# Value projections with the activations stationary, in a two-block transformer kernel

## The reference

```python
qkv = jnp.einsum('bsd,de->bse', x, w_qkv).reshape(b, s, 3, h, dh)
...
p = jax.nn.softmax(...)
return (... + jnp.einsum('bhqk,bhkd->bhqd', p_own, v_own))
```

## Time and profile before

| | |
|---|---|
| median of 3 runs | 819.25 us (818.97 to 820.73) |
| span of the profiled execution, first to last instruction | 817.3 us |
| median above the span | 1.95 us |
| TensorE busy (matmuls) | 802.3 us, 98% |
| VectorE busy | 644.4 us, 79% |
| ScalarE busy | 487.0 us, 60% |

### The profile page before, as it was taken

One profiled execution on the slowest core, in us unless ns is written; L12 is line 12 of the kernel. 1 busy time (PEld: TensorE's weight loads), 2 busy tenths in 40 slices (PEclk: granted clock), 3 DMA queues, 4 the chain that ended last, 5 costly groups with the idle time before them and its releaser, 6 DMA issues.

```text
span 817.3 us, 16917 instructions
## 1 busy us (share of the span) xinstructions
PE 802.3 (98%) x6862; PEld 780.7 (96%) x6862; DVE 644.4 (79%) x1333; ACT 487.0 (60%) x1015; POOL 21.2 (3%) x53
## 2 busy tenths in 40 slices
PE   7999999999999999999999999899999999999998
PEld 7999998999999999999999999889889999999998
DVE  5788887888899887999988786977667896775551
ACT  6754566767767565756554556665655775555440
POOL 1000000000000000000000000700000000000000
PEclk9999999999999999999999999999999999999999
DMA  8777673765565998489998887545334578665540
GB/s 290 260 234 226 200 267 128 235 199 188 189 225 166 324 308 286 144 295 336 361 333 292 288 263 222 167 134 175 120 118 156 156 249 274 207 199 194 194 155 27
DMA packets 150013, 179.44 MB, mean 220 GB/s; under 512 B 5680, under 2 KB 139568, under 8 KB 149936
## 3 DMA queue, kind: packets, MB, share of 16 engines
q1 hardware_dynamic: 147680, 177.22, 65.8%
q10 hardware_dynamic: 1232, 1.11, 0.4%
q0 software_dynamic: 1024, 0.03, 0.1%
HBM read 177.27 MB, written 1.05 MB: 218 GB/s over the span
## 4 chain that ended last, share of the span: by engine, by line
PE 77%; DVE 4%; ACT 2%; issue 1%; DVEq 0%; ACTq 0%
PE bank L1349 24%; PE bank L1352 24%; PE bank L1353 24%; DVE wlo L970 1%; PE bank L1451 1%; PE bank L1439 1%; PE bank L1468 0%; PE bank L1370 0%; PE bank L1402 0%; DVE yb L1010 0%; PE bank L1418 0%; DVE A L1021 0%; ACT B L748 0%; PE bank L1395 0%; ACT sq L768 0%
## 5 line engine op out<-in xcount | busy, mean ns | idle before, releaser
L970 DVE TENSOR_TENSOR wlo<-raw,whi 128x512 fp32r<-128x512 f32 x528 | 342.7, 683 | 69.4 <-ACT whi L727 68.7
L727 ACT ACTIVATE whi<-raw 128x512 fp32r<-128x512 f32 x528 | 307.3, 622 | 97.1 <-PE bank L1353 85.2
L1349 PE MATMUL bank<-A,whi 128*128 128x256 f32 x1264 | 357.3, 283 | 3.4 <-DVE wlo L970 2.6
L1352 PE MATMUL bank<-A,whi 128*128 128x256 f32 x1264 | 350.6, 277 | 0.1
L1353 PE MATMUL bank<-A,wlo 128*128 128x256 f32 x1264 | 350.2, 277 | 0.0
L1349 PEld LDWEIGHTS bank<-A,whi 128*128 128x128 f32 x1264 | 237.7, 188 | 6.5 <-DVE wlo L970 3.5
L1352 PEld LDWEIGHTS bank<-A,whi 128*128 128x128 f32 x1264 | 237.7, 188 | 1.2 <-issue 1.0
L1353 PEld LDWEIGHTS bank<-A,wlo 128*128 128x128 f32 x1264 | 237.8, 188 | 0.0
L1349 PE MATMUL bank<-Hhi,whi 128*128 128x256 f32 x528 | 146.2, 277 | 0.0
L1353 PE MATMUL bank<-Hhi,wlo 128*128 128x256 f32 x528 | 145.9, 276 | 0.0
L1352 PE MATMUL bank<-Hlo,whi 128*128 128x256 f32 x528 | 145.9, 276 | 0.0
(11 more groups left out here) (150 smaller groups left out, 811.0 us busy)
## 6 DMA issues: line engine op xcount, KB each, us to landing
mring<-in_w_mod SPq DMA_DIRECT2D x72, 512.0 KB, 6.4
raw<-in_ffn_w_up SPq DMA_DIRECT2D x22, 1024.0 KB, 5.1
raw<-in_w_gate SPq DMA_DIRECT2D x22, 1024.0 KB, 5.7
raw<-in_w_up SPq DMA_DIRECT2D x22, 1024.0 KB, 6.0
raw<-in_w_down SPq DMA_DIRECT2D x16, 1024.0 KB, 5.4
raw<-in_w_in SPq DMA_DIRECT2D x12, 1024.0 KB, 5.4
raw<-in_moba_w_qkv SPq DMA_DIRECT2D x11, 1024.0 KB, 5.5
raw<-in_ffn_w_down SPq DMA_DIRECT2D x8, 1024.0 KB, 6.2
```

The lines of the kernel that those rows point to most:

```text
L727: act.activation(whi[:, i % SPL, k0:k1, 0:width], raw[:, i % RAW, k0:k1, 0:width], ACT.Copy).then_inc(s_whi, 1)
L970: dve.tensor_tensor(lo, raw[:, i % RAW, k0:k1, 0:width], hi.bitcast(F32), ALU.subtract).then_inc(s_wlo, 1)
L1349: pe.matmul(o, hi, xh, start=kg == 0 and not (j and halved(g)), stop=False)
L1352: pe.matmul(o, hi, xl, start=False, stop=False)
```

## The change

The value groups are computed with the operands exchanged: the activations of 128 tokens are stationary and 256 columns of weights move, so that the result is token-major and VectorE evicts it straight into Vn. The step vturn is gone on both engines. In qkv1 the root of the norm is now needed as one number for each partition; root_columns gets it, once, as the diagonal of the broadcast root. In qkv3 the slabs at 1024 (sb values) and 1536 (first fox queries) change places, so that no value group is unnormed. The query group in fourth place is now the unnormed one.

```diff
-PAD_H = 168 - PAD_C
+PAD_H = 166 - PAD_C
...
-         + slabs_of("qkv", w_in, KD, [0, 512, 1024, 1536, 2048, 2560, 256, 768, 1280, 1792, 2304, 2816])),
+         + slabs_of("qkv", w_in, KD, [0, 512, 1536, 1024, 2048, 2560, 256, 768, 1280, 1792, 2304, 2816])),
...
+def is_value(ph, tag, c0):
+
+    return tag == "qkv" and qkv_base(ph, c0) >= 16
...
-                elif kind == "vturn":
-                    st.put("vturn", ph, at)
-                    v_ready.update((at - 16, at - 15))
...
                 if base >= 16:
-                    pending.append(("vturn", ph, base, turns[0] + (1 if base == 22 else 2)))
+                    v_ready.update((base - 16, base - 15))
...
+        rcol = sb("rcol", [P, 2])
...
-            def v_turned(ph, tile):
-                need.wait_ge(s_tpe, t_use["vturn", ph, tile] + 1)
-                c = (tile - 16) * P
-                src = banks[T_BANK][:, 0:2 * S].rearrange("p (a c) -> p a c", a=2)
-                act.activation(Vn[:, :, c:c + S], src, ACT.Copy).then_inc(s_vn, 1)
...
+            def root_columns():
+
+                have_r("qkv1")
+                need.wait_ge(s_const, n_const)
+                for i in range(2):
+                    dve.scalar_tensor_tensor(out=tmp[:, i, 0:P], in0=Rr[:, 0, i * P:(i + 1) * P], scalar=1.0, in1=identf[:, :],
+                                             op0=ALU.mult, op1=ALU.mult, accum_out=rcol[:, i:i + 1]).then_inc(s_rcol, 1)
+
+            def values_out(g):
+
+                ph, _, c0 = groups[g]
+                c = (qkv_base(ph, c0) - 16) * P
+                if ph == "qkv1" and c == 0:
+                    root_columns()
+                for i in range(2):
+                    o = Vn[:, i, c:c + C]
+                    if ph == "qkv1":
+                        need.wait_ge(s_rcol, 2)
+                        ins = dve.tensor_scalar(o, at(g, i), rcol[:, i:i + 1], None, ALU.mult)
+                    else:
+                        ins = dve.tensor_copy(o, at(g, i))
+                ins.then_inc(s_evicted, 1)
...
+                if is_value(ph, tag, c0):
+                    for j in range(2):
+                        o, q = at(g, j), slice(j * P, (j + 1) * P)
+                        hi, lo = whi[:, i % SPL, kt, :], wlo[:, i % SPL, kt, :]
+                        pe.matmul(o, xh[:, q], hi, start=kg == 0 and not (j and halved(g)), stop=False)
+                        pe.matmul(o, xl[:, q], hi, start=False, stop=False)
+                        ins = pe.matmul(o, xh[:, q], lo, start=False, stop=final and (j == 1 or not halved(g)))
...
-                need.wait_ge(s_vn, nth("vturn", ph, 16 + h // 4 * 2))
+                emptied(need, qkv_group[ph, 16 + h // 4 * 2])
...
-            def v_turn(ph, tile):
-                b = banks[T_BANK]
-                emptied(need, qkv_group[ph, tile])
-                need.wait_ge(s_const, n_const)
-                t_free("vturn", ph, tile)
-                for i in range(2):
-                    for h in range(2):
-                        c = h * S + i * P
-                        ins = pe.transpose(b[:, c:c + P], QKV[:, tile + i, h * P:(h + 1) * P], identf[:, :])
-                ins.then_inc(s_tpe, 1)
```

More of the change, by code:

```diff
@@ L244, in advance @@
             if age == LAST_AGE:
-                while h // 2 not in v_ready:
-                    pend(force=True)
+                assert h // 2 in v_ready
                 st.put("values", n)
@@ L510, in build_program @@
         s_tpe, s_tfree, s_w, s_val, s_ohi, s_olo = (sem(n) for n in ("s_tpe", "s_tfree", "s_w", "s_val", "s_ohi", "s_olo"))
-        s_lsum, s_vn = sem("s_lsum"), sem("s_vn")
+        s_lsum, s_rcol = sem("s_lsum"), sem("s_rcol")
         s_gq, s_qsq, s_qln, s_qr, s_qkn = (sem(n) for n in ("s_gq", "s_qsq", "s_qln", "s_qr", "s_qkn"))
         s_f1, s_f2, s_f3, s_f4, s_flo, s_fsplit, s_fset = (sem(n) for n in ("s_f1", "s_f2", "s_f3", "s_f4", "s_flo", "s_fsplit", "s_fset"))
-        t_use = {step: k for k, step in enumerate(s for s in st.list if s[0] in ("turn", "later", "vturn", "qkn"))}
+        t_use = {step: k for k, step in enumerate(s for s in st.list if s[0] in ("turn", "later", "qkn"))}
         soft = {n: k + 1 for k, n in enumerate(m for m, h in enumerate(heads) if h[0] != "sb")}
@@ L953, in _ @@
                        "ccol": condition, "evict": evict, "fpart": forget, "scores": first_passes, "turn": turned, "later": later,
-                       "values": values, "vturn": v_turned, "qkn": qk_norm}
+                       "values": values, "qkn": qk_norm}
             for step in st.list:
@@ L1081, in evict @@
                     need.wait_ge(s_chunk, chunk_of_group(g))
-                if tag == "qkv" and ph == "qkv1":
+                if is_value(ph, tag, c0):
+                    values_out(g)
+                elif tag == "qkv" and ph == "qkv1":
                     have_r(ph)
@@ L1343, in multiply @@
                     pe.matmul(banks[NORM_BANK][:, 511:512], meanf[:, :], meanf[:, 0:1], start=True, stop=True)
+                if is_value(ph, tag, c0):
+                    for j in range(2):
[4 more added lines that the diff above has]
+                        ins = pe.matmul(o, xh[:, q], lo, start=False, stop=final and (j == 1 or not halved(g)))
+                    if kt % 2 == 1:
+                        ins.then_inc(s_chunk, 1)
+                    return
                 for j in range(1 if tag == "f" else 2):
@@ L1425, in t_free @@
                     was = next(s for s, u in t_use.items() if u == k - 1)
-                    if was[0] == "vturn":
-                        need.wait_ge(s_vn, nth(*was))
-                    elif was[0] == "qkn":
+                    if was[0] == "qkn":
                         need.wait_ge(s_qln, nth(*was))
@@ L1471, in _ @@
             part_of = {"warm": warm, "mm": multiply, "norm": norm, "scores": scores, "turn": turn, "later": later,
-                       "values": values, "vturn": v_turn, "qkn": qk_norm}
+                       "values": values, "qkn": qk_norm}
             for step in st.list:
```

## The result

The changed kernel is slower: 829.39 us (827.96 to 830.12) against 820.32 for the kernel before measured beside it, ratio 1.0113 (95% 1.0097 to 1.0129). The span of its profiled execution is 827.9 us against 817.3, so 10.6 us are to be found. (The medians are 9.1 apart: the profiled execution, at 830.12 us, is the slowest of the five.)

A forecast was written before the change was run, and what follows sets the result against it. TensorE, busy 98% at full clock, was taken as the bound. -3.6 us for removed turns, 0 for swapped matmuls and +4.6 for the order gave +1.0 on 819.25: 820.2 us, range 815.9 to 823.0 (its own 818.6 to 821.9).

The forecast's parts named there:

- Part 1, the turns: Value turns removed from TensorE in qkv1 and qkv3: seven sum to -3.6 us, bounds -2.4 and -4.5.
- Tile 22 of qkv3: Its removed value turn in qkv3, a gap of 0.99 us on TensorE, was to save 0.8 us.
- Tile 18: Its removed value turn in qkv3 was to save 0, TensorE only waiting longer for head 27's sum.
- Part 2, the swapped matmuls: 384 value matmuls in qkv1 and qkv3 with operands exchanged, and their eviction: 0 us, pace bounds 1.9 us either way.
- Part 3, the order: In qkv3, swapping slabs 1024 and 1536 makes TensorE wait for head 16's sum: net +4.6 us, bounds +0.3 and +5.1.
- later 16: TensorE's step in qkv3 that needs head 16's sum: to start at 535.7 instead of 530.64, +5.06 us.
- The wait for the sum: In qkv3, TensorE was to wait 4.3 us for VectorE's sum of head 16.
- The clock rival: Clock falls at the wait ahead of later 16 in qkv3: 2.1 to 4.3 us lost, 822.3 to 824.5; chance 0.12.
- the pace: Swapped value matmuls in qkv1 and qkv3 at 0.113 or 0.118 us each: 1.9 us either way, taken as 0.

The follow-up runs named there:

- e1: The changed kernel with PAD_H 6 columns smaller, so that Hhi and the buffers behind it stand at their old addresses; 821.5 us, ratio 1.0017.
- e3: e1 with query tile 4's step qkn due 6 attends after its eviction instead of 2; 819.9 us, ratio 0.9998.
- e4: e3 with the Square of query tile 4 moved on ScalarE to the next value group's eviction; 815.24 us, ratio 0.9941.
- e5: The kernel before with Hhi and what lies behind it 64 bytes further on; 831.23 us, ratio 1.0142.
- e11: e4 with the rows of B 288 instead of 258 columns apart; 819.35 us, ratio 1.0001.
- e6: e4 with the rows of B 272 instead of 258 columns apart; 815.75 us, ratio 0.9947.
- e7: e3 with 26 matmuls on constants put into TensorE's wait ahead of later 16; 819.38 us, ratio 0.9992.

## Why the prediction was wrong

**The step that failed** is one that the sum doesn't have. I costed every edit that issues instructions and passed over the one that issues none: `rcol` and the smaller padding. Hhi moved by 32 bytes against the weights, and the down phases lost 7.7 us (profiled; 7.9 by the medians of the changed kernel and e1). The prediction reckoned with two paces, 0.118 and 0.113, for the swapped matmuls alone. Its trace had both, and I left open what sets them. For the down phases that question was worth 7.9 us, where the whole sum came to +1.0.

**Part 1, the turns: right.** Forecast -2.63 for qkv1 (2.43 and 0.2); measured -2.86 by the start of o1. Tile 22 of qkv3: forecast -0.8, measured -0.7 (8.47 us late at the start of o3, 7.81 at its second slab). Tile 18 gave nothing, as forecast.

**Part 2, the swapped matmuls: right.** In qkv1 the value slabs run at 0.114 to 0.115 us, in qkv3 at 0.116 to 0.118 (530.42 to 530.54 above), inside the two known paces and with no net cost that the comparison of slab starts shows. root_columns cost nothing: slab 256 starts at 29.29 instead of 29.33.

**Part 3, the order: right in mechanism and time.** later 16 was forecast at 535.7 in the old time. It starts at 538.35, and the changed kernel was already 2.62 us late at slab 1536, which gives 535.73. VectorE's wait of 4.06 us for the Exp, the six passes ahead of it and the wait for the Square are there. The blk matmul starts at 526.72 in the old time (526.8 forecast) and the main matmuls at 527.28 (527.25). The wait for the sum is 3.67 us where I had 4.3: the matmul behind blk takes 0.52 us to the next start (529.90 to 530.42), the others run at 0.117, and the profile counts idle time only from a matmul's modelled end. The end is the same. By slab 2560 the term is +5.75 instead of +4.6.

**The clock rival came true in kind**, with its chance of 0.12, but not at its price. The 1.15 us between 4.6 and 5.75 lie where the clock stood at 0.51, and the rival had 2.1 to 4.3. That 1.15 is the clock's is argued from the place: no run separates it in the changed kernel. What a low clock costs depends on where it falls. In e3 work is waiting, and it cost 1.4 to 2.4 us. In e1's profiled execution it fell behind the wait for the Square, with 12 matmuls in 526 to 528 instead of some 17, and the later wait of 2.11 us swallowed the delay, so nothing of it is seen at later 16. e1's own clock rows:

```profile
524.00:526.00 2.00, 2.00 (x7) 1.37 (x8) 0.69 (x1) 1.94 (x5) 2.00 (x6) 0.67 1.09 364
526.00:528.00 2.00, 2.00 (x12) 2.00 (x11) 0.00 (x0) 1.94 (x5) 2.00 (x6) 0.50 0.14 9
```

The Trainium skill ("TensorE: Matmul & The Clock Gate", section "Why this matters for your kernels") warns against long idle stretches between bursts of matmuls; the traces agree for the longest waits, with a clock of 0.50 after waits of 3.67 and 3.78 us and 1.00 throughout after e4's 1.42. In between, the length of the wait alone doesn't decide: the wait of 2.19 us for the Square left the clock at 1.00 in the changed kernel (529.34), but in e1 the same wait, ending at 523.88, was followed by 0.67 and 0.50; and in e5's profiled execution the clock fell during the second of two waits, 1.62 and 1.19 us, ahead of up1.

Without the shift the prediction would have been near: e1 measured 821.5 against 820.2 forecast, inside its own range of 818.6 to 821.9, and 0.17% above the kernel before, 1.4 us, where +1.0 was forecast. That range is 0.2% to either side. It isn't what the bounds named for it give: part 1's alone span 819.3 to 821.4, and the pace adds 1.9 either way.

## What to carry to other kernels

Count an added or resized buffer as an edit of the matmuls that read the buffers behind it. Compare the addresses of the moving operands before and after, and the matmuls in 40 us of a stretch that the change doesn't touch. Where a step is moved, look for every part of it on every in-order engine, the eviction's Square as much as the step itself: e3 moved one and won 1.6 us, e4 moved both and won 4.7 more, part of it because TensorE's wait grew short enough for the clock to stay up.

## What the runs showed that was not expected

- At full clock and without a break, fp32r matmuls of 128x128 by 256 columns ran at 0.1133, 0.118 to 0.119 or 0.120 us each in the down phases, by the distance of the moving buffer from the buffers that stayed, modulo 256 bytes: 192 gives the first, 64, 128 and 224 the second, 0 the third. Why, the runs don't tell.
- A slow rhythm can run over well-placed operands: in e11 it lasted ten slabs, in up2 and again in up4, and in e6 two. What starts and ends it is open.
- A float32 matmul of 128x128 by 128 columns took 0.22 us in a run of its own kind (e7) and left two records in the profile, 52 for 26, so a count in a line of the timeline isn't always a count of the kernel's matmuls.
- A wait of 3.8 us brought some 7 us at the lower clock (e3: 0.72, 0.50, 0.50 and 0.57 in the four stretches from 527 to 535), about 2 of them still in the wait, and it cost 1.4 to 2.4 us.
